# Prompt memory units of the first layer moved from behind the heads into heads one to five, in one PSUM bank, with units paired by column half

## The reference

```
z  = rmsnorm(h) @ a_w_in          # columns: q | k | v | gate (6 heads x 128 each), then 4 memory queries x 64
q, k = rope(q), rope(k) * 128**-0.5
per head, chunks of 128 rows:     # retention
  o = (q k^T * decay_mask) v + (q * q_decay) S ;  S = chunk_decay * S + (k * k_decay)^T v
mix = head_groupnorm(o) * silu(gate)
om  = softmax(qm @ mem_k^T * 64**-0.5) @ mem_v      # 4 memory heads of width 64, 256 memory rows
h   = h + concat(mix, om) @ a_w_out
h   = h + square(relu(rmsnorm(h) @ w_up)) @ w_down
```

## Time and profile before

| what | value |
|---|---|
| median of 3 runs | 1651.38 us |
| the profiled execution's own time | 1651.49 us |
| its span | 1649.7 us |
| granted TensorE clock, mean | 0.97 |
| TensorE busy | 1547.9 us, 94% of the span |
| VectorE busy | 827.9 us, 50% |
| ScalarE busy | 565.6 us, 34% |

### The profile page before, as it was taken

How to read it: one execution, slowest core, us unless ns; L and a number is a source line. 1 busy time by engine, 2 the same in 40 slices (tenths; PEclk the granted TensorE clock), 3 DMA queues, 4 the chain that set the end, 5 groups by cost and what they waited for, 6 DMA issues and landing times.

```text
span 1649.7 us, 28864 instructions
## 1 busy us (share of the span) xinstructions
PE 1547.9 (94%) x11443; PEld 1438.9 (87%) x11443; DVE 827.9 (50%) x1288; ACT 565.6 (34%) x876; POOL 50.4 (3%) x76
## 2 busy tenths in 40 slices
PE   3899999779999999999999789999899999999998
PEld 3889999569999999999988457766799999999998
DVE  4846777635533433334576645655454334343344
ACT  4532222323422313223443135555243223132234
POOL 1120000010000000000001000000000000000000
PEclk8999999889999999999999889999999999999999
DMA  6543333122232332222324303543122223323221
GB/s 193 167 141 92 92 92 92 56 82 77 77 90 77 90 88 78 82 83 77 90 80 120 107 11 93 145 121 99 46 83 70 84 81 89 87 76 89 76 89 58
DMA packets 229383, 149.34 MB, mean 91 GB/s; under 512 B 11121, under 2 KB 222466, under 8 KB 229282
## 3 DMA queue, kind: packets, MB, share of 16 engines
q1 hardware_dynamic: 218802, 122.57, 25.8%
q0 software_dynamic: 6032, 20.28, 4.1%
q10 hardware_dynamic: 4448, 5.11, 0.9%
HBM read 140.26 MB, written 7.68 MB: 90 GB/s over the span
## 4 chain that ended last, share of the span: by engine, by line
PE 72%; DVE 5%; ACT 2%; issue 1%; ACTq 0%; DVEq 0%
PE ps L572 57%; PE ps L1064 3%; PE ps L1022 2%; PE ps L1091 2%; PE ps L1005 1%; PE ps L932 1%; PE ps L967 1%; PE ps L968 1%; DVE t L1858 1%; DVE wl L1566 1%; DVE rstd L1585 1%; PE ps L935 1%; PE ps L962 1%; PE ps L1000 0%; ACT wh L1172 0%
## 5 line engine op out<-in xcount | busy, mean ns | idle before, releaser
L572 PE MATMUL ps<-xh,wh 128*128 128x288 f32 x1542 | 334.5, 299 | 15.1 <-DVE wl L1566 15.1
L572 PE MATMUL ps<-mh,wh 128*128 128x288 f32 (+1 forms) x1424 | 325.3, 297 | 17.0 <-DVE wl L1566 13.7
L572 PE MATMUL ps<-xh,wl 128*128 128x288 f32 x1542 | 329.7, 295 | 0.0
L572 PE MATMUL ps<-xl,wh 128*128 128x288 f32 x1542 | 329.5, 295 | 0.0
L572 PE MATMUL ps<-ml,wh 128*128 128x288 f32 (+1 forms) x1424 | 322.9, 296 | 0.0
L572 PE MATMUL ps<-mh,wl 128*128 128x288 f32 (+1 forms) x1424 | 322.8, 295 | 0.0
L1172 ACT ACTIVATE wh<-raw 128x1024 fp32r<-128x1024 f32 (+1 forms) x195 | 202.1, 1036 | 286.0 <-PE ps L572 268.3
L1566 DVE TENSOR_TENSOR wl<-raw,wh 128x1024 fp32r<-128x1024 f32 (+1 forms) x195 | 233.0, 1195 | 74.0 <-ACT wh L1172 72.7
L572 PEld LDWEIGHTS ps<-xh,wh 128*128 128x128 f32 x1542 | 248.3, 190 | 20.6 <-DVE wl L1566 17.3
L572 PEld LDWEIGHTS ps<-mh,wh 128*128 128x128 f32 x1424 | 237.5, 190 | 19.9 <-DVE wl L1566 14.5
L572 PEld LDWEIGHTS ps<-xl,wh 128*128 128x128 f32 x1542 | 248.6, 189 | 0.0
(11 more groups left out here) (290 smaller groups left out, 1341.7 us busy)
## 6 DMA issues: line engine op xcount, KB each, us to landing
raw<-in_w_up SPq DMA_DIRECT2D x64, 512.0 KB, 4.0
raw<-in_w_down SPq DMA_DIRECT2D x64, 512.0 KB, 3.6
pages<-in_cache_mla SPq DMA_DIRECT2D x128, 160.0 KB, 2.2
raw<-in_a_w_in SPq DMA_DIRECT2D x26, 512.0 KB, 3.8
memkc<-in_cache_mem_k POOLq DMA_DIRECT2D x16, 256.0 KB, 4.6
memvc<-in_cache_mem_v POOLq DMA_DIRECT2D x16, 256.0 KB, 5.7
raw<-in_a_w_out SPq DMA_DIRECT2D x8, 512.0 KB, 3.7
raw<-in_b_w_out SPq DMA_DIRECT2D x8, 512.0 KB, 3.7
```

The source lines that it names most:

```text
L572: last = mm(ps[:, 2 * (m % 2) + c, 0:n], w[:, s, kk, :], x(kk, col, n), start=(kk == 0 and nth == 0), stop=(kk == k - 1 and nth == 2))
```

## The change

- `unit_of(h, part)` places unit u of the first layer in two neighbouring parts of a head: unit 0 in parts 2 and 3 of head 1, units 1 to 6 in heads 2 to 4, two per head (parts 0 and 1, parts 2 and 3), unit 7 in parts 0 and 1 of head 5.
- In the even part a unit's first score matmul stands behind four K-tiles, its second behind `ret_rows` (part 0) or behind the fifth K-tile (part 2). VectorE's maximum and normalisation stand ahead of the tile's own eviction, and in part 2 so ahead of the statistics of retention. In the odd part the transposes stand behind four K-tiles and the values behind the tile. A unit uses bank 7 for everything, and one buffer each for E and PT, which lie in `ss` and `sq`.
- A unit is now row block u//2 and heads 2b and 2b+1, with b = u%2: its two score matmuls read different 64 partitions and are ordered by a semaphore, its value matmuls alternate between the two halves of the output partitions.
- Retention gives up bank 7: `ret_rows` moves to the middle of part 0, its scores become `ret_scores` behind part 0 in bank 4, `ret_kv` moves to the middle of part 1, its state update becomes `ret_update` behind part 1; `ret_out` and `ret_back` move from the middle to behind parts 2 and 3. The gated result is written over `onorm` instead of `t1`.
- Behind the last projection tile, the last head's retention is woven into the first two output tiles, whose K-tile 5 (that head) comes last (`out_part`).
- In the second layer the units take the same pairing; `unit_half` is the first score matmul on its own, and each unit is evicted by itself instead of every second.

```diff
+def unit_place(q):
+
+    if q < MEM_UNITS:
+        return q // 2, H_RET + q % 2
+    return (q - MEM_UNITS) // H_MLA, (q - MEM_UNITS) % H_MLA
+
+
+def unit_of(h, part):
+
+    t = 4 * (h - 1) + part - 2
+    return t // 2 if 0 <= t < 2 * MEM_UNITS else None
 
...
+            def unit_scores_a(u):
+
+                i, b = u // 2, u % 2
+                pe.wait_ge(*((me_lo, u) if u else (ms_lo, 2)))
+                mm(ps[:, 7, 0:256], qm[0:64, b, P * i:P * i + P], kT[0:64, 0, b, :], start=True, stop=True).then_inc(me_half, 1)
+
+            def unit_half_a(u):
+
+                i, b = u // 2, u % 2
+                pe.wait_ge(me_half, u + 1)
+                mm(ps[:, 7, 256:512], qm[64:P, b, P * i:P * i + P], kT[64:P, 0, b, :], start=True, stop=True).then_inc(me_sc, 1)
+
+            def unit_turn_a(u):
+
+                pe.wait_ge(me_norm, u + 1)
+                for r in range(2):
+                    for a in range(2):
+                        last = pe.transpose(ps[:, 7, P * (2 * r + a):P * (2 * r + a) + P], mem[0]["E"][:, a, P * r:P * r + P], ident[:, :])
+                last.then_inc(me_tr, 1)
+
+            def unit_values_a(u):
+
+                pe.wait_ge(me_pt, u + 1)
+                for r in range(2):
+                    for a in range(2):
+                        h = a + 2 * (u % 2)
+                        last = mm(ps[64 * a:64 * a + 64, 7, 0:P], mrow[:, 0, r, MEM_W + 64 * h:MEM_W + 64 * h + 64],
+                                  mem[0]["PT"][:, r, P * a:P * a + P], start=(r == 0), stop=(r == 1))
+                last.then_inc(me_pv, 1)
...
+                mm(ps[0:NS, 6, 256:256 + NS], zk[:, SEQ:ROWS], zq[:, SEQ:ROWS], start=True, stop=True).then_inc(r_rows, 1)
+
+            def ret_scores(h):
+                zq, zk = (z[:, h % 2, x, :] for x in range(2))
+                pe.wait_ge(r_act, 2 * h + 1)
                 for n in range(RT):
-                    last = mm(ps[:, 7, P * n:P * n + P], zk[:, P * n:P * n + P], zq[:, P * n:P * n + P], start=True, stop=True)
-                last.then_inc(r_rows, 1)
+                    last = mm(ps[:, 4, P * n:P * n + P], zk[:, P * n:P * n + P], zq[:, P * n:P * n + P], start=True, stop=True)
+                last.then_inc(r_sc, 1)
...
+
+            def ret_update(h):
+                pe.wait_ge(r_masked, h + 1)
+                pe.wait_ge(r_st, h + 1)
+                for half in range(2):
+                    rows = slice(32 * half, 32 * half + 32)
+                    last = mm(ps[:, 4 + half, :], krs[rows, :], vexp[rows, :, :].rearrange("p b e -> p (b e)"), start=True, stop=True)
+                last.then_inc(r_up, 1)
 
             def ret_out(h):
...
-            def z_tile(h, part, middle=None):
-                for ks in (range(KD // 2), range(KD // 2, KD)):
+            def z_tile(h, part, middle=None, u=None):
+                for ks in (range(KD // 2), range(KD // 2, KD // 2 + 1), range(KD // 2 + 1, KD)):
                     dense(M_Z + 2 + 4 * h + part, tiles(xh), tiles(xl), part=ks)
                     if middle and 0 in ks:
                         middle(h - 1)
+                    if u is not None and KD // 2 in ks:
+                        unit_half_a(u)
...
-            last_head = {2: ret_rows, 4: ret_kv, 6: ret_out, 9: ret_back}
-            for k in range(2, 12):
-                mem_step(0, k)
-                if k in last_head:
-                    last_head[k](H_RET - 1)
+                for part in range(4):
+                    u = unit_of(h, part)
+
+                    def middle(h):
+                        if h == 0 and part == 0:
+                            sample_back(0, 1)
+                        if u is not None:
+                            (unit_scores_a, unit_turn_a)[part % 2](u)
+                        if part < 2:
+                            (ret_rows, ret_kv)[part](h)
+                        if u is not None and part == 0:
+                            unit_half_a(u)
+
+                    z_tile(h, part, middle, u if part == 2 else None)
+                    (ret_scores, ret_update, ret_out, ret_back)[part](h - 1)
+                    if u is not None and part % 2:
+                        unit_values_a(u)
+
+            def out_part(j, *part):
+                dense(M_OUT[0] + j, tiles(mh), tiles(ml), part=part, final=H_RET - 1)
+
+            last = H_RET - 1
+            ret_rows(last)
+            pe.wait_ge(me_lo, MEM_UNITS)
+            pe.wait_ge(r_lo, last)
+            out_part(0, 0, 1, 2)
+            ret_scores(last)
+            out_part(0, 3, 4)
+            ret_kv(last)
+            out_part(0, 6, 7)
+            ret_update(last)
+            out_part(1, 0, 1, 2)
+            ret_out(last)
+            out_part(1, 3, 4, 6, 7)
+            ret_back(last)
+            pe.wait_ge(r_lo, H_RET)
+            for j in range(2):
+                out_part(j, last)
 
             def out_and_mlp(layer):
 
 
-                if layer == 0:
-                    pe.wait_ge(me_lo, RT)
-                    pe.wait_ge(ms_lo, 2)
-                    for part in (range(H_RET - 1), range(H_RET - 1, KD)):
-                        for j in range(2):
...
+            def unit_max_a(u):
+
+                dve.wait_ge(me_sc, u + 1)
+                do(dve.reduce_max(vec[:, 0:2], ps[:, 7, :].rearrange("p (b m) -> p b m", b=2), AX))
+                do(ts(vec[:, 4:6], vec[:, 0:2], -MEM_SCALE, None, ALU.mult), C[me_max])
+
+            def unit_norm_a(u):
+
+                dve.wait_ge(me_exp, u + 1)
+                do(dve.reciprocal(vec[:, 12:14], vec[:, 8:10]))
+                E = mem[0]["E"]
+                do(tt(E[:, :, :], E[:, :, :], vec[:, 12:14].unsqueeze(2).to_broadcast([P, 2, NMEM]), ALU.mult), C[me_norm])
+
+            def unit_values_a(u):
+
+                i, h = u // 2, H_RET + u % 2
+                dve.wait_ge(me_hi, u + 1)
+                do(tt(ml[:, h, P * i:P * i + P], ps[:, 7, 0:P], mh[:, h, P * i:P * i + P].bitcast(F32), ALU.subtract), C[me_lo])
 
...
-                    last_head[k](H_RET - 1)
+                for part in range(4):
+                    u = unit_of(h, part)
+
+                    def middle(h):
+                        if h == 0 and part == 0:
+                            sample_low(0, 1)
+                        if u is not None and part % 2 == 0:
+                            unit_max_a(u)
+                        if part < 2:
+                            (ret_rows, ret_kv)[part](h)
+                        if u is not None and part % 2 == 0:
+                            unit_norm_a(u)
+
+                    def end(h):
+                        (ret_scores, ret_update, ret_out, ret_back)[part](h)
+                        if u is not None and part % 2:
+                            unit_values_a(u)
+
+                    z_tile(h, part, middle, end)
+
+            last = H_RET - 1
+            w_tail(M_OUT[0] + 1)
+            for step in (ret_rows, ret_scores, ret_kv, ret_update, ret_out, ret_back):
+                step(last)
 
             def add_residual(m, j, i=None):
                 dve.wait_ge(acc_ready, at(m + 1, i))
@@ -1991,16 +2037,11 @@
 
...
+            def unit_half(q):
+
+                if not 0 <= q < MEM_UNITS:
                     return
                 if q >= 2:
                     pe.wait_ge(u_exp, q - 1)
+                i, b = q // 2, q % 2
+                mm(ps[:, q % 2, 0:256], qm[0:64, b, P * i:P * i + P], kT[0:64, 1, b, :], start=True, stop=True).then_inc(u_half, 1)
+
...
-                    a = q % 2
-                    for b in range(2):
-                        h = a + 2 * b
-                        for r in range(2):
-                            last = mm(ps[64 * a:64 * a + 64, 3, P * b:P * b + P], mrow[:, 1, r, MEM_W + 64 * h:MEM_W + 64 * h + 64],
-                                      mPT[:, q % 2, 256 * r + P * b:256 * r + P * b + P], start=(r == 0), stop=(r == 1))
+                    for r in range(2):
+                        for a in range(2):
+                            h = a + 2 * (q % 2)
+                            last = mm(ps[64 * a:64 * a + 64, 3, 0:P], mrow[:, 1, r, MEM_W + 64 * h:MEM_W + 64 * h + 64],```

VectorE around the step from head 3 to head 4, before. `wl` is a split weight, `t_65<-ps,rstd` the eviction of the gate tile, L1740 and L1742 the gated result of the head before, L1761 the gate.

```order
L1590 TENSOR_TENSOR z<-ps,rstd 128x576
L1566 TENSOR_TENSOR wl<-raw,wh 128x1024
L1740 SCALAR_TENSOR_TENSOR t_65<-ps,z 128x576
L1742 TENSOR_TENSOR ml<-t_65,mh 128x576
L1590 TENSOR_TENSOR t_65<-ps,rstd 128x576
L1761 SCALAR_TENSOR_TENSOR z<-t_66,t_65 128x576
L1566 TENSOR_TENSOR wl<-raw,wh 128x1024
```

More of the change, by code:

```diff
@@ L319, in build @@
         s_out = sem("s_out")
-        r_rows, r_act, r_dve, r_kv, r_state, r_o = (
-            sem(f"r_{n}") for n in ("rows", "act", "dve", "kv", "state", "o"))
+        r_rows, r_act, r_dve, r_sc, r_masked, r_kv, r_st, r_up, r_state, r_o = (
```

(17 more changed lines are left out.)

253 lines of the change are left out of this document (84 added, 169 removed).

## The result

The changed kernel takes 1632.57 us (median, 1631.58 to 1633.83); the kernel before took 1652.47 us (1650.91 to 1654.24) in the runs beside it. The ratio is 0.988, 95% interval 0.986 to 0.989: 20 us faster. The forecast was 1636 us. The two profiled executions took 1651.49 and 1633.83 us, so that the traces can account for 17.7 us; the other 2.2 us are the choice of the executions, the one before being 1.0 us under its median here and the one after 1.3 us over.

The account below looks back on a forecast made before the run. TensorE, busy 94% of the span, was taken to bound the kernel, with time to win in a 60.5 us chain between engines. 1651.5 + 23.2 (heads) - 36.6 (behind them) - 2.0 (second layer) = 1636.1 us; range 1630 to 1642.

Parts of the forecast that it names:

- Units and cuts, 5.3 us a head: In first-layer heads: two units' scores, transposes and values, plus 0.5 us for cuts in the dense stream, add 5.3 us.
- The values overlap, 0.6 us: In a unit's value matmuls: alternating halves overlap, so the eight instructions take 0.6 us, between 0.5 and 1.02.
- The wait in part 0, 1.1 us: At the start of the next head: TensorE waits 1.1 us for the unit's low part; in part 2, 0.3 us.
- A head 41 us, the last projection tile at 321: In the first layer: a head takes about 41 us and the last projection tile ends 23.2 us later, at about 321.
- The term for head 5, +2.3: In head 5, with one unit and one wait, `ret_back` leaving the tile (-0.8): 2.3 us longer.
- The wait ahead of `ret_back`, 3.8 us, and a clock at 0.5 behind it: Behind the last projection tile: TensorE waits 3.8 us for the last head's statistics, until E+27.2, then transposes at half clock.
- One sign of the forecast: In the profile after: no 20 us window between 120 and 340 us has TensorE under 17 us busy.
- The third output tile at E + 39.5: Behind the last projection tile's end E: the third output tile starts at E+39.5, against E+76.1 before, -36.6 us.
- Second layer, -2.0: In the second layer's units: values and scores change by 8 x (-0.4 + 0.15) = -2.0 us, between -4 and +1.
- The sum: Whole kernel: 1651.5 + 23.2 - 36.6 - 2.0 = 1636.1 us.
- the fall of the clock inside the heads: Rival, in parts 0 and 2: longer waits for the unit's low part bring the clock down, 1664 us; chance 0.05.
- The rival that the waits vanish: Rival: no waits in heads 2 to 5, no fall of the clock, halves drain-free, 1626 us; chance 0.17.

Follow-up runs that it names:

- `values_serial`: Changed kernel, but in both layers a unit's value matmuls do one half of the output partitions, then the other, instead of alternating: 1633.74 us, ratio to before 0.989.
- `early_low`: Changed kernel, but in part 3 ScalarE evicts the unit ahead of the Tanh and VectorE makes its low part ahead of the gated result: 1627.34 us.
- `tail_early`: Changed kernel, but three K-tiles of the output projection go ahead of `ret_rows`, other K-tiles are respread, and VectorE splits the second output weight later: 1628.67 us.
- `halves_same`: Changed kernel, but in the second layer first score halves of neighbouring units, reading the same 64 partitions, stand side by side: 1634.78 us, ratio to before 0.989.
- `late_low`: Changed kernel, but VectorE makes the low part of units 0, 2, 4 and 6 only in the next head's part 0: 1651.69 us, ratio to before 0.999.
- `both`: Changed kernel with the edits of `early_low` and `tail_early` together: 1623.03 us, ratio to before 0.982.

## Why the prediction was right

1. *Units and cuts, 5.3 us a head.* The head took 40.80 us: 34.66 less 0.58, plus 1.18, plus 5.54. The units were cheaper than forecast: a half 0.63 (227.62 to 228.25), transposes 0.36 (237.09 to 237.45) or 0.43, values 0.58, so some 2.2 us for 2.4. The cuts were dearer, about 1.1 us for 0.5, and for a part of it the rows say why: the last dense pair ahead of a score half occupies 0.45 us (227.17 to 227.62), the last one ahead of the transposes only 0.26 (236.83 to 237.09), so the change to the half-height form costs too. Another 0.3 us stand ahead of `ret_back` (0.56 us for the pair from 240.47 to 241.03). I had priced only what comes behind a cut. The two errors, -0.4 and +0.6, offset each other in part, and that is luck.
2. *The values overlap, 0.6 us.* 0.58 to 0.59. The size was right and a part of the reason wrong: it spoke of alternating like the page values, and `values_serial` shows that alternation has no part in it.
3. *The wait in part 0, 1.1 us.* 1.18, and for the reason given, shown by `early_low`. In part 2 I had 0.3 and there was none.
4. *A head 41 us, the last projection tile at 321.* 40.80 and 320.3, 22.6 us later for 23.2. The term for head 5, +2.3, does not follow from its parts (2.4 + 0.5 + 1.1 - 0.8 = 3.2, or 2.6 with the 0.6 us of wait taken off); heads 1 and 5 together took 4.2 us for 4.6.
5. *The output projection at E + 6.3* (E is the end of the last projection tile). 326.64 is E + 6.3.
6. *The wait ahead of `ret_back`, 3.8 us, and a clock at 0.5 behind it.* 3.78 us. It came at E + 30.2 and not at 27.2: the clock had also fallen once in the waits before it. The prediction gave that fall 2.5 us and left it out of the sum. `tail_early` takes those waits away, and the clock stays up. One sign of the forecast failed: the window 318 to 338 us has 16.10 us of TensorE and not 17, since the waits of 0.58, 2.07 and 1.25 us lie in it.
7. *The third output tile at E + 39.5.* 40.9: 3.0 later at `ret_back`, 1.6 less behind it (10.7 us to the third tile for 12.3), of which 1.1 is the way from `ret_back` to K-tile 5 (3.98 us, 350.58 to 354.56, for 5.1). Here too two errors offset each other.
8. *Second layer, -2.0.* -3.2 in the stretch of the units, and up to -4.6 with the fall of the clock behind it, if that belongs here. This term was mis-sized. 0.8 us of the difference are the score halves that run together (`halves_same`), which the term had not counted: I had only asked what a half costs by itself.
9. *The sum.* -15.4 forecast, -17.7 in the profiled executions: -12.5 for -13.4 at the third tile, -0.5 between the layers, -3.2 for -2.0, and -1.4 from a fall of the clock that only one of the two executions had. The mechanisms of the first layer were the ones forecast; that 1636 came within 3.4 us of the median owes something to errors of both signs and to which execution of the kernel before had been profiled.

Of the rivals, the fall of the clock inside the heads did not come true, and it was a real one: waits of 3.2 us in the same places bring it about (`late_low`), those of 1.2 do not. The prediction had put the turn at about 2.5, which lies between and was not tried in the heads. Elsewhere the length of one wait did not decide alone: behind 1.30 us the clock was down in two traces and up in ten. The rival that the waits vanish was wrong for this kernel, and is what `both` makes of it.

## What to carry to other kernels

Small chained work costs little in the gaps of a dense stream if each step's answer is ready when the stream comes back to it; so lay out the queue of the engine that answers, not only that of TensorE: here one placement on VectorE decided between 20 us and nothing. Price a wait as rows of the same stretch show it: in these heads waits of 1.2 us cost themselves, and waits of 3.2 us also the slow work behind them. And before building, look for what can go ahead of the step that is waited for or of the one that waits: one move of each kind gave 9.5 us more.

## What the runs showed of the hardware that I had not expected

- Four value matmuls (eight instructions) take 0.59 us when they write both halves of the output partitions, in both orders tried, against 1.02 us in one half.
- Two matmuls on different 64 input partitions and different banks started within 0.01 us of each other though they belong to different units: four instructions in 0.63 us (972.67 to 973.30), four on the same partitions in 1.06 (969.98 to 971.04).
- Four waits of 1.2 us in the heads left the clock at 1.00. Four of 3.2 us brought it down, and 8.2 us more of waiting cost 19.2.
- A wait of 1.30 us in the second layer was followed by matmuls at 1.2 GHz in the two traces with the old units, and at 2.4 GHz in the ten with the new ones.
- The same order of instructions behind the last projection tile took 38.7 or 40.9 us, by where in it the clock fell and rose.
